# Norm sums in every partition by one full-precision matmul with ones, in place of column sums, diagonals and spreading matmuls

## What is computed

```python
def rmsnorm(x, g):
    x32 = x.astype(jnp.float32)
    y = x32 * lax.rsqrt(jnp.mean(x32 * x32, axis=-1, keepdims=True) + EPS)
    return y.astype(x.dtype) * g

def layernorm(x, g, b):
    mu = jnp.mean(x32, axis=-1, keepdims=True)
    xc = x32 - mu
    y = xc * lax.rsqrt(jnp.mean(xc * xc, axis=-1, keepdims=True) + EPS)
```

## Time and profile before

| | |
|---|---|
| median of the runs | 1988.05 us |
| profiled execution, its own time | the span of 1984.8 us from its first to its last instruction; no other time is given for it |
| TensorE busy (matmuls) | 1928.0 us, 9052 records |
| VectorE busy | 1174.5 us |
| ScalarE busy | 747.0 us |
| GpSimd busy | 1009.2 us |
| mean granted TensorE clock | 0.995 |

### The profile page before, as it was taken

How to read it: one execution, slowest core, us unless ns; L and a number is a source line. 1 busy time by engine, 2 the same in 40 slices (tenths; PEclk the granted TensorE clock), 3 DMA queues, 4 the chain that set the end, 5 groups by cost and what they waited for, 6 DMA issues and landing times.

```text
span 1984.8 us, 24859 instructions
## 1 busy us (share of the span) xinstructions
PE 1928.0 (97%) x9052; PEld 1593.7 (80%) x9052; DVE 1174.5 (59%) x2098; ACT 747.0 (38%) x1096; POOL 1009.2 (51%) x1271
## 2 busy tenths in 40 slices
PE   7999899998999999999999999999999999999997
PEld 5788788787788887888888888788878888888886
DVE  7987778977776667554332335666676553233235
ACT  5444534435324545223231323345453333223230
POOL 6344264352643336755645646533447566465652
PEclk9999999999999999999999999999999999999998
DMA  4221132221222122223232222222222222222221
GB/s 178 92 82 64 57 106 92 82 85 43 97 86 85 64 86 86 106 86 106 91 106 88 104 95 96 86 86 82 89 78 93 106 86 92 100 104 88 106 85 64
DMA packets 28058, 178.92 MB, mean 90 GB/s; under 512 B 3872, under 2 KB 4000, under 8 KB 7456
## 3 DMA queue, kind: packets, MB, share of 16 engines
q1 hardware_dynamic: 24192, 169.88, 24.1%
q10 hardware_dynamic: 3744, 7.45, 1.1%
HBM read 175.22 MB, written 2.10 MB: 89 GB/s over the span
## 4 chain that ended last, share of the span: by engine, by line
PE 72%; DVE 16%; issue 6%; ACT 3%; POOL 2%; ACTq 0%; DVEq 0%
PE bank L534 66%; PE bank L555 3%; DVE bank L1832 3%; POOL W_lo L506 2%; DVE PR L1753 1%; DVE PR L1774 1%; DVE PT_lo L1625 1%; ACT PR L1203 1%; PE bank L585 1%; PE bank L597 1%; DVE Y_lo L1625 1%; ACT PT_hi L1173 1%; PE bank L576 1%; PE bank L566 1%; ACT W_hi L1169 0%
## 5 line engine op out<-in xcount | busy, mean ns | idle before, releaser
L506 POOL TENSOR_TENSOR W_lo<-W_raw,W_hi 128x256 fp32r<-128x256 f32 (+1 forms) x1228 | 985.3, 838 | 925.8 <-ACT W_hi L1169 925.8
L534 PE MATMUL bank<-H_hi,W_hi 128*128 128x512 f32 x1264 | 499.8, 395 | 4.9 <-DVE PRE L1903 1.9
L534 PE MATMUL bank<-H_hi,W_lo 128*128 128x512 f32 x1264 | 492.9, 390 | 0.0
L534 PE MATMUL bank<-H_lo,W_hi 128*128 128x512 f32 x1264 | 491.9, 389 | 0.0
L534 PE MATMUL bank<-Y_hi,W_hi 128*128 128x512 f32 x972 | 383.6, 395 | 6.9 <-DVE Y_lo L1625 2.1
L534 PE MATMUL bank<-Y_hi,W_lo 128*128 128x512 f32 x972 | 379.6, 391 | 0.0
L534 PE MATMUL bank<-Y_lo,W_hi 128*128 128x512 f32 x972 | 379.5, 390 | 0.0
L1169 ACT ACTIVATE W_hi<-W_raw 128x2048 fp32r<-128x2048 f32 (+2 forms) x159 | 295.8, 1861 | 201.9 <-DMA W_raw<-in_stream 196.5
L534 PEld LDWEIGHTS bank<-H_hi,W_hi 128*128 128x128 f32 x1264 | 237.4, 188 | 54.5 <-DVE Y_lo L2181 1.8
L534 PEld LDWEIGHTS bank<-H_hi,W_lo 128*128 128x128 f32 x1264 | 237.2, 188 | 50.6
L534 PEld LDWEIGHTS bank<-H_lo,W_hi 128*128 128x128 f32 x1264 | 237.6, 188 | 47.3
(11 more groups left out here) (305 smaller groups left out, 2324.9 us busy)
## 6 DMA issues: line engine op xcount, KB each, us to landing
W_raw<-in_stream SPq DMA_DIRECT2D x160, 1024.0 KB, 4.8
BT<-in_bias ACTq DMA_DIRECT2D x8, 320.0 KB, 3.2
X<-in_x ACTq DMA_DIRECT2D x4, 512.0 KB, 7.3
out<-X SPq DMA_DIRECT2D x8, 256.0 KB, 2.2
BT<-in_rope ACTq DMA_DIRECT2D x2, 512.0 KB, 3.6
MC<-in_causal ACTq DMA_DIRECT2D x2, 256.0 KB, 3.4
MS<-in_window ACTq DMA_DIRECT2D x1, 321.0 KB, 8.2
NM<-in_columns ACTq DMA_DIRECT2D x1, 320.0 KB, 9.4
```

The source lines that it names most:

```text
L506: ins = nc.gpsimd.tensor_tensor(W[1][:, s, part], W_raw[:, s, part], W[0][:, s, part].bitcast(F32), ALU.subtract)
L534: mm = pe.matmul(out, lhs[a], rhs[b], start=(not begun and k == 0 and a == 0 and b == 0), stop=(not more and k == n - 1 and a == 1), skip_ ...
```

## The change

Each sum is now one matmul with all of ones (128x128) as the stationary operand and the 128x512 accumulator moving, so that the sums stand in every partition at once (two matmuls where two accumulators are added). ScalarE's root and VectorE's reciprocal work on 128x512. Diagonals and spreads go. The copies RB2 and RB go too, since the root or the reciprocal writes there; RB1's copy moves into the loop of scaled tiles (k = 5). The kv and q means become 128x512 passes with EPA, now 128x512 as well.

```diff
+    def pe_totals(pe, b, l, name, parts, bank=NB, ready=None):
         count, at = ready or (b.acc, l)
         pe.wait_ge(count.sem, count.at(at, name))
+        for n, acc in enumerate(parts):
+            to = bank[n] if isinstance(bank, tuple) else bank
+            own_bank = isinstance(bank, tuple)
+            mm = pe.matmul(to[:, :], ones[:, :], acc, start=(own_bank or n == 0),
+                           stop=(own_bank or n == len(parts) - 1), skip_group_check=True)
         mm.then_inc(b.ss.sem, 1)
...
-            for mm in by_tiles(pe, slot_of(1, l, 0), RAW, first_tiles(0, "n"), dict(zip((2, 6), norms)) if l else {}):
+            for mm in by_tiles(pe, slot_of(1, l, 0), RAW, first_tiles(0, "n"), {2: totals} if l else {}):
...
-                for mm in by_tiles(pe, slot_of(1, l, 1), RAW, first_tiles(1, ""), dict(zip((4, 6), norms)), out=TB):
+                for mm in by_tiles(pe, slot_of(1, l, 1), RAW, first_tiles(1, ""), {4: totals}, out=TB):
...
-                if i == LN_STEP + 3:
-                    pe_spread(pe, b1, l, "var")
...
-                               {2: lambda: pe_sums(pe, b2, l, "n", (ACC2,)),
-                                6: lambda: pe_spread(pe, b2, l, "n", bank=OB)} if l else
-                               {6: lambda: pe_sums(pe, b2, l, "n", (ACC2, ACCG))}):
+                               {2: lambda: pe_totals(pe, b2, l, "n", (ACC2,), OB)} if l else
+                               {6: lambda: pe_totals(pe, b2, l, "n", (ACC2, ACCG), (NB, OB))}):
...
                 if name == "q00":
-                    if not l:
-                        pe_spread(pe, b2, l, "n", bank=OB)
-                        pe_spread(pe, bf, 0, "between", TMP[:, 1, :], TB[0])
-                    pe_sums(pe, b2, l, "kv", (ACC2,))
-                if name == "q01":
-                    pe_spread(pe, b2, l, "kv")
+                    pe_totals(pe, b2, l, "kv", (ACC2,))
                 if name == "lr0":
-                    pe_sums(pe, b2, l, "q", (ACC2,))
-            pe_spread(pe, b2, l, "q")
+                    pe_totals(pe, b2, l, "q", (ACC2,))
...
+        def root_of_total(b, l, name, n, bank=NB, out=None):
+
+            root_table()
             act.wait_ge(b.ss.sem, b.ss.at(l, name))
             act.wait_ge(*own.last(1))
-            nc.scalar.activation(NR[:, 0:4], NB[:, 0:4], ACT.Sqrt, bias=EPSC[:, :], scale=1.0 / n) \
+            nc.scalar.activation(bank[:, :] if out is None else out, bank[:, :], ACT.Sqrt, bias=EPSC[:, :], scale=1.0 / n) \
                 .then_inc(b.rt.sem, own.event(b.rt, l, name))
+
+        def root_of_mean(b, l, name, out, ready=None):
+
+            root_table()
+            act.wait_ge(*(ready or (b.ms.sem, b.ms.at(l, name))))
+            act.wait_ge(*own.last(1))
+            nc.scalar.activation(out, TMP[:, 0, :], ACT.Sqrt).then_inc(b.rt.sem, own.event(b.rt, l, name))
...
-            root(b2, l, "n", 4 if l else 8)
+            if l:
+                root_of_total(b2, l, "n", D, OB, RB2[:, :])
+            else:
+                root_of_mean(b2, l, "n", RB2[:, :], (bf.ms.sem, bf.ms.at(0, "n")))
+                act.wait_ge(*own.last(1))
+                nc.scalar.activation(NB[:, :], NB[:, :], ACT.Sqrt, bias=EPSC[:, :], scale=1.0 / D) \
+                    .then_inc(bf.rt.sem, own.event(bf.rt, 0, "between"))
...
-        def diagonals(b, l, name, spread=True):
+        def inverse(b, l, name, out, root):
 
             dve.wait_ge(b.rt.sem, b.rt.at(l, name))
             dve.wait_ge(*own.last(1))
-            nc.vector.reciprocal(NR[:, 0:4], NR[:, 0:4]).then_inc(dve_step, own.step())
-            diagonal(b, l, name, TMP[:, 0, :], 0)
-            if spread:
-                dve.wait_ge(b.bc.sem, b.bc.at(l, name))
...
+            nc.vector.reciprocal(out, root).then_inc(dve_step, own.step())
...
-        def mean(b, l, name, n=D, eps=None):
+        def mean(b, l, name, n):
...
+            nc.vector.scalar_tensor_tensor(TMP[:, 0, :], NB[:, :], 1.0 / n, EPA, ALU.mult, ALU.add) \
+                .then_inc(b.ms.sem, own.event(b.ms, l, name))
+
+        def scale_of_total(b, l, name):
...
+            nc.vector.tensor_scalar(NB[:, :], NB[:, :], 1.0 / D, EPS, ALU.mult, ALU.add).then_inc(dve_step, own.step())
             dve.wait_ge(*own.last(0))
...
+            nc.vector.reciprocal(RB, NB[:, :]).then_inc(dve_step, own.step())
...
-            mean(b1, l, "n")
-            diagonals(b1, l, "n")
-            dve.wait_ge(*own.last(1))
-            nc.vector.tensor_copy(RB1[:, :], NB[:, :]).then_inc(dve_step, own.step())
+            inverse(b1, l, "n", NB[:, :], NB[:, :])
...
+                if k == 5:
+                    dve.wait_ge(*own.last(1))
+                    nc.vector.tensor_copy(RB1[:, :], NB[:, :]).then_inc(dve_step, own.step())
...
-                    diagonals(b1, l, "var", spread=False)
+                    inverse(b1, l, "var", NB[:, :], NB[:, :])
...
-            if l:
-                mean(b2, l, "n")
-            else:
+            if not l:
...
+                nc.vector.tensor_scalar(EPA, NB[:, :], EPS / D, EPS * EPS, ALU.mult, ALU.add) \
                     .then_inc(dve_step, own.step())
                 dve.wait_ge(*own.last(0))
...
+                nc.vector.scalar_tensor_tensor(TMP[:, 0, :], OB[:, :], 1.0 / D, EPA, ALU.mult, ALU.add) \
+                    .then_inc(bf.ms.sem, own.event(bf.ms, 0, "n"))
                 dve.wait_ge(*own.last(0))
...
+                nc.vector.tensor_scalar(EPA, TMP[:, 0, :], EPS, None, ALU.mult).then_inc(dve_step, own.step())
...
             for n in range(2):
                 squares(ACC2, GT[:, n, :], n == 0)
+            inverse(b2, l, "n", RB2[:, :], RB2[:, :])
+            if l:
+                dve.wait_ge(*own.last(1))
+                nc.vector.tensor_scalar(EPA, OB[:, :], EPS / D, EPS * EPS, ALU.mult, ALU.add) \
+                    .then_inc(dve_step, own.step())
+            else:
+                inverse(bf, 0, "between", TB[0][:, :], NB[:, :])
             mark(b2.acc, l, "kv")
-            dve.wait_ge(b2.bc.sem, b2.bc.at(l, "n"))
-            dve.wait_ge(*own.last(1))
-            nc.vector.tensor_copy(RB2[:, :], OB[:, :]).then_inc(dve_step, own.step())
...
             q_latent(0)
-            diagonals(b2, l, "kv", spread=False)
-            dve.wait_ge(b2.bc.sem, b2.bc.at(l, "kv"))
+            inverse(b2, l, "kv", NB[:, :], NB[:, :])
...
-            spread_scale(b2, l, "e")
+            scale_of_total(b2, l, "e")
...
-        mean(bf, 0, "n")
-        diagonals(bf, 0, "n")
+        inverse(bf, 0, "n", OB[:, :], OB[:, :])
```

More of the change, by code:

```diff
@@ L327, in _build @@
     b2.ss = Count(sem("norm_sum2"), 0, [("", 1, norms2)])
-    b2.ms = Count(sem("norm_mean2"), 0, [("", 1, ["n", "kv", "q"])])
+    b2.ms = Count(sem("norm_mean2"), 0, [("", 1, ["kv", "q"])])
     b2.rt = Count(sem("norm_root2"), 0, [("", 1, ["n", "kv", "q"])])
-    b2.dg = Count(sem("norm_diag2"), 0, [("", 1, norms2)])
-    b2.bc = Count(sem("norm_spread2"), 0, [("", 1, norms2)])
     b2.layer = Count(sem("layer2"), 1, [("", 1, ["end"])])
     bf = Block()
-    bf.ss, bf.ms, bf.rt = (Count(sem(f"norm_{n}F"), 0, [("", 1, ["n"])]) for n in ("sum", "mean", "root"))
-    bf.dg, bf.bc = (Count(sem(f"norm_{n}F"), 0, [("", 1, ["between", "n"])]) for n in ("diag", "spread"))
+    bf.ss = Count(sem("norm_sumF"), 0, [("", 1, ["n"])])
+    bf.ms = Count(sem("norm_meanF"), 0, [("", 1, ["n"])])
+    bf.rt = Count(sem("norm_rootF"), 0, [("", 1, ["between", "n"])])
     final = Count(sem("final"), 0, [("", 1, [str(k) for k in range(KT)])])
@@ L858, in _ @@
                 if i == LN_STEP + 2:
-                    pe_sums(pe, b1, l, "var", (ACC1,), last=HA[:, 0, PAD_A:PAD_A + S])
+                    pe_totals(pe, b1, l, "var", (ACC1[:, :], HA[:, 0, PAD_A:PAD_A + S]))
             begin_unit(1, l, 15)
@@ L2226, in _ @@
             receive("lr0", GT[:, 12, :], "")
-            mean(b2, l, "q", 3 * P, EPA[:, :])
-            diagonals(b2, l, "q", spread=False)
+            mean(b2, l, "q", 3 * P)
+            inverse(b2, l, "q", NB[:, :], NB[:, :])
             dve.wait_ge(b2.hi.sem, b2.hi.at(l, "kr"))
```

96 lines of the change are left out of this document (14 added, 82 removed).

## The result

The changed kernel takes **1991.88 us** (median of 7 runs, 1990.22 to 1994.45), the kernel before on the same chip 1987.9 (median of 7, 1986.28 to 1988.16): ratio **1.0024, 95% interval 1.0015 to 1.0032**. Forecast were 1991.0, +3.0 on the kernel before; measured are +4.0. The profiled execution of the changed kernel took 1994.45 with a span of 1992.6. It is the slowest of its 7, and it is set here against the one of before with 1984.8; so the shifts between the two traces add up to 7.8 us, about twice what the medians differ by. (The shift at a place is how much later the same matmul of TensorE starts in the one trace than in the trace of before; it is given with the time of the trace of before.) What scatters is TensorE's clock: the two executions with a mean granted clock of 0.995 took 1990.2 and 1990.3, the two with 0.990 took 1994.2 and 1994.5.

A forecast was written before the change was run, and what follows sets the result against it. TensorE, busy 97%, bounds most of the kernel; VectorE and ScalarE bound places like the convolution's norm. Terms summed to +2.3, plus 0.7 for the clock: +3.0, span 1987.8, median 1991.0 us; range 1984 to 2001.

The forecast's parts named there:

- rival B: All 128x512 reciprocals run at eight passes, 4.4 us each: +13 on top, 2004 us; chance 0.12.
- R: Time of one 128x512 reciprocal on VectorE, taken as 3.2 us; 11 us of total per microsecond above that.
- Rivals A: A cheap reciprocal, as fast as a copy (0.7 us), so the removed spreads pay: -14, 1974 us; chance 0.08.
- var, +2.0 per layer: Convolution's norm, both layers: later root and reciprocal delay the softmax step and TensorE's output projection; +4.0 us in all.
- Rival C: VectorE's later 1.64 us idle time hides the convolution norm's delay, layer 0's latents stay level: -3, 1985 us; chance 0.08.
- First block, input norms: First attention block: layer 0 -0.1 us, its spread off the chain; layer 1 -0.9 us, TensorE's chain including the spread.
- Latents, layer 0, +1.4: Second block: two reciprocals ahead of the kv-sum signal stall TensorE; first scaled q at 594.8 against 593.39 us.
- The stall: Second block, layer 0: TensorE waits 4.3 us ahead of the kv sums, for a signal behind two reciprocals.
- Latents, layer 1, -0.5: Second block: 1.8 us stall at the kv sums, VectorE just in time at the q norm, spread's 0.9 counts.
- Feed-forward norm, -0.9 each: Both layers: spread removed from never-idle TensorE pays in full; VectorE's extra 1 us is hidden; -1.8 us in all.
- Last norm, +0.3: Final norm, all serial: root and reciprocal put the first output tile at 1977.0 against 1976.75 us.
- Clock, +0.7: Behind layer 0's 4.3 us stall the granted clock may drop to 0.50, costing up to 1.7 us; 0.7 taken.

The follow-up runs named there:

- e9: The changed kernel with the reciprocal of the convolution's norm done three times in a row in both layers; 2005.23 us, ratio 1.0094 to the kernel before.
- e3: The changed kernel with the signal for the kv sums moved ahead of the reciprocals in both layers of the second block; 1993.27 us, ratio 1.0027.
- e6: e3 with latent q01 ahead of the scaled kv tiles and, in layer 0, the "between" reciprocal and scalings moved behind the first scaled q; 1988.19 us.
- e10: The changed kernel with the second block's four norms (n, between, kv, q) put back as before the change; 1990.79 us, ratio 1.0012.
- e1: The changed kernel with each of its 14 reciprocals of 128x512 replaced by a tensor_scalar of the same operands; 1971.16 us, ratio 0.9917.
- e2: The changed kernel with the convolution's norm alone put back as before (column sums, 128x4 root and reciprocal, diagonals, spread); 1989.18 us, ratio 1.0007.
- e7: e6 with the convolution's norm put back as before the change; 1983.66 us, ratio 0.9978 to the kernel before.
- e13: e7 with the "between" reciprocal cut into four pieces and the scalings of X moved to the second and third head pairs; 1983.02 us, ratio 0.9977.
- e11: The changed kernel with the reciprocal of the feed-forward norm done twice in a row in both layers; 2004.94 us, ratio 1.0086.

## Why the prediction was right, and where it was wrong

The total, its sign and its mechanism held; several terms did not, and partly cancelled. That +3.0 came within 1 us of the measured +4.0 is partly luck: the latents of layer 1 cost 2.1 more than forecast, the low clocks in the first block were not in the sum, and neither were the 1.7 us gained in the product of MRG. Two slips in the working change little: its terms add up to +2.4, not +2.3, and rival B's eight passes make 4.3, not 4.4.

- **R.** 3.2 was taken, 3.355 measured, within the 3.0 to 3.5 that the small rows gave. At 11 us per microsecond the difference is +1.7, so with R right the sum would have said +4.7, against +4.0. Rivals A (0.7) and B (4.4) fall with that row. The Trainium skill (VectorE: DVE Perf Modes, "First, the fixed hardware budget") gives the reciprocal a repeat count of 8; these rows do not bear it out as eight times a copy's time, which would be 4.3 us: 3.355 less the fixed 0.17 is 6.1 times the 0.52 that a copy takes beyond it.
- **var, +2.0 per layer.** 1.98 by the traces in layer 0 and 2.3 in layer 1, and e9's 6.8 per layer for 6.7 shows the slope. Rival C (taken up by the idle time ahead of 221.21) falls: that idle time moved along.
- **First block, input norms.** Layer 0 was forecast at -0.1. The first scaled tile came 0.43 later (34.67), but TensorE's sums had begun 0.72 later already (29.52 against 28.80), ahead of anything that was changed in the norm. On TensorE's matmuls the shift is +0.70 ahead of the norm and +0.65 at 90 us, so -0.05. Layer 1, forecast -0.9: the shift went from +3.29 to +2.38, so -0.9.
- **Latents, layer 0, +1.4.** The stall was right (4.10 for 4.3). The first scaled q came 2.55 later instead of 1.4 (shift +9.64 against +7.09 ahead of the stage; from the first copy of G it is 3.2, but that copy came 0.7 earlier, as forecast). Part is R (four of them, 0.6), and part the clock, which the forecast carried as a separate 0.7: the sum behind the stall (two records) took 1.55 us, that of layer 1 1.12. TensorE's matmuls came 2.1 later, as the 1.4 and the 0.7 together say. e3 and e6 correct the reading: the prediction put the cost down to the mark, which stood behind two reciprocals, and to the stall there. With the mark first the stalls moved on, the clock fell further and nothing was gained; with VectorE's work taken out of the stretch 7.8 us were. What costs is VectorE's volume ahead of the first scaled q; the mark only chose where TensorE waited.
- **Latents, layer 1, -0.5: this step failed.** It came at +1.64 (shift +7.33 ahead, +8.97 at the first scaled q). "At the q norm VectorE is just in time" left no room for what VectorE met: passes of 0.69 that took 2.14 and 1.83, and with them a wait of 2.02 at kr, beside 2.40 instead of 1.8 at the mark. Both long passes overlap GpSimd's weight splits and end 0.55 us behind the last of them (1277.79 against 1277.24, 1293.78 against 1293.23). In this trace the 185 passes of that kind (TENSOR_TENSOR of 128x512, no bank among its operands) with no GpSimd instruction beside them all took 0.68 to 0.70; of the 219 beside one 161 took 1.0 or more. That ties the delay to GpSimd; no run moved its splits alone. The low clock plays no part here.
- **Feed-forward norm, -0.9 each.** Right in size (-0.98 by the trace in layer 0, -0.96 in layer 1) and wrong in its cover. "TensorE waits for ScalarE's relu of a chunk only two chunks on", and "if that cover were gone, 1 us": ScalarE's queue carries the next weight split behind that relu, the slack was 0.2 to 0.4 us, and one more reciprocal cost 5.9 us per layer by the traces. By that slack, an estimate, TensorE would have begun to wait there from R = 3.6 to 3.8 on, and rival B would have been worse than its 2004.
- **Last norm, +0.3.** 0.04: from the sums to the first output tile 7.05 us (1977.52 to 1984.57), where it was 7.01.
- **Clock, +0.7.** The granted clock was 0.91 behind the 4.10 us stall, as said. Its scatter from run to run, some 4 us of time between 0.990 and 0.995, is as large as the whole effect, and the forecast did not weigh it. Nor is it mere scatter. Of the kernels with var's long reciprocal as in the change (the changed one, e3, e6, e10) 28 of 36 executions had a mean clock of 0.992 or less; of those with a short one or none there (e1, e2, e7, e13) 3 of 36, and of the kernel before 6 of 63. At 0.995 the changed kernel took 1990.2 and 1990.3, so about 1.7 of its +4.0 go with the clock.

Open: what in the steps of var puts the clock down, and why the product of MRG is faster without NR. Either is as large as a term of the sum, and no experiment changed it alone.

## What to carry to other kernels

To spread a small result over a tile before a slow elementwise operation is to pay that operation on every column: here 14 reciprocals went from 0.18 to 3.36 us, for 14 spreads of 0.9 on TensorE, and what decided each place was whose time was on the path, not which engine was busier on average. When an engine is late, take work out of the stretch before moving signals within it: a moved signal moved the stall, and 8.9 us of work moved into a stretch where VectorE was 70% busy still cost 5.0. An operation hidden "two chunks on" must be followed through the in-order queue that waits for it, down to the last thing behind it; doing it twice shows the slack. And before a run that puts a part back is read as the price of that part, the stages that it did not touch should be compared as well: here one of them hid 1.7 us.

## What the runs showed of the hardware that was not expected

- A reciprocal of 128x512 takes 3.34 to 3.36 us on average from PSUM and from SBUF alike, though a copy-like pass takes 0.69.
- A stall of TensorE cost more than itself: 3.95 us idle brought a window of 20 us at a granted clock of 0.91, and the two such stalls of e11 came to 11.7 us of time by the shifts, 13.1 by the medians.
- The same pass of VectorE on 128x512, both inputs in SBUF, took between 0.69 and 2.14 us within one kernel, and 0.70 at most where GpSimd ran nothing beside it.
- The same 192 matmuls took 43.9 to 44.0 us in the seven kernels without the tile NR and 44.7 to 44.8 in the seven with it.
